# The RWKV chunk stage's preparation up to the directed keys, made once in the projection (hybrid retention and RWKV-7 layer, Trainium2)

## The reference, cut to what matters

```python
kk = heads(k * k_k); kk = kk * rsqrt(sum(kk * kk) + 1e-12)
u = w0[d] + tanh(wd) @ w2[d]                  # 64 -> 512, both directions
w = exp(-exp(-softplus(-u) - 0.5))            # = exp(-exp(-0.5) * sigmoid(u))
a = sigmoid(a0[d] + ad @ a2[d])
k_dir = k * (1.0 + (a - 1.0) * k_a)
# the scan takes w, k_dir, v, kk, a and r; later bonus = sum(r * k_dir * r_k) * v
```

## Time and profile before

| | us |
|---|---|
| median of 3 runs (4056.05 to 4069.73) | 4059.08 |
| the profiled execution | 4071.43 |
| its span | 4069.6 |

### The profile page before, as it was taken

How to read it: one execution, slowest core, us unless ns; L and a number is a source line. 1 busy time by engine, 2 the same in 40 slices (tenths; PEclk the granted TensorE clock), 3 DMA queues, 4 the chain that set the end, 5 groups by cost and what they waited for, 6 DMA issues and landing times. The chain is left out here.

```text
span 4069.6 us, 94464 instructions
## 1 busy us (share of the span) xinstructions
PE 3694.0 (91%) x39914; PEld 3087.6 (76%) x39914; DVE 2247.2 (55%) x3650; ACT 1892.5 (47%) x3029; POOL 671.5 (16%) x637
## 2 busy tenths in 40 slices
PE   7999999999978888888887978996699999999993
PEld 6878878888867777777776867785588888888883
DVE  5532533434337777777776865555444544454545
ACT  5533534433336666666565443332244444444443
POOL 1000000000012222222220333200011111111111
PEclk9999999999989999999999989998799999999997
DMA  7655565555442223322324366655366666666667
GB/s 260 199 188 183 179 198 155 154 157 158 149 145 73 69 78 81 81 79 74 96 65 124 111 221 225 202 168 189 134 206 217 214 217 212 214 206 214 212 212 299
DMA packets 378746, 673.49 MB, mean 165 GB/s; under 512 B 90428, under 2 KB 261540, under 8 KB 360712
## 3 DMA queue, kind: packets, MB, share of 16 engines
q1 hardware_dynamic: 351368, 580.69, 44.0%
q0 software_dynamic: 27008, 87.46, 7.4%
HBM read 524.89 MB, written 143.15 MB: 164 GB/s over the span
## 5 line engine op out<-in xcount | busy, mean ns | idle before, releaser
L113 PE MATMUL fro__acc<-fro__hT_hi,fro__wh 128*128 128x512 f32 (+1 forms) x1608 | 624.9, 389 | 11.8 <-DVE fro__hT_lo L2695 8.9
L114 PE MATMUL fro__acc<-fro__hT_hi,fro__wl 128*128 128x512 f32 (+1 forms) x1608 | 612.9, 381 | 0.0
L115 PE MATMUL fro__acc<-fro__hT_lo,fro__wh 128*128 128x512 f32 (+1 forms) x1608 | 612.8, 381 | 0.0
L2112 DVE TENSOR_TENSOR fin__wl<-fin__raw,fin__wh 128x4096 fp32r<-128x4096 f32 x96 | 424.7, 4424 | 316.8 <-ACT fin__wh L2056 316.8
L2701 DVE TENSOR_TENSOR fro__wl<-prj__w,fro__wh 128x1024 fp32r<-128x1024 f32 x201 | 246.3, 1225 | 637.6 <-ACT fro__wh L2484 637.6
L2056 ACT ACTIVATE fin__wh<-fin__raw 128x4096 fp32r<-128x4096 f32 x96 | 348.4, 3629 | 190.8 <-PE exp__acc L115 190.3
L113 PE MATMUL exp__acc<-fin__wh,exp__xh 128*128 128x512 f32 x1024 | 399.9, 390 | 0.8 <-DVE exp__xl L2117 0.8
L115 PE MATMUL exp__acc<-fin__wl,exp__xh 128*128 128x512 f32 x1024 | 398.5, 389 | 0.0
L114 PE MATMUL exp__acc<-fin__wh,exp__xl 128*128 128x512 f32 x1024 | 398.4, 389 | 0.0
L113 PEld LDWEIGHTS fro__acc<-fro__hT_hi,fro__wh 128*128 128x128 f32 x1608 | 303.7, 189 | 77.7 <-issue 22.2
L114 PEld LDWEIGHTS fro__acc<-fro__hT_hi,fro__wl 128*128 128x128 f32 x1608 | 303.8, 189 | 59.1 <-issue 3.6
(11 more groups left out here) (462 smaller groups left out, 7570.1 us busy)
## 6 DMA issues: line engine op xcount, KB each, us to landing
fin__raw<-in_w_x SPq DMA_DIRECT2D x96, 2048.0 KB
prj__w<-in_w_z SPq DMA_DIRECT2D x201, 512.0 KB, 4.1
s_zT<-fro__pool SPq DMA_DIRECT2D x128, 256.0 KB, 4.5
fro__wm<-in_w_mod POOLq DMA_DIRECT2D x16, 1024.0 KB, 5.8
mix__gate<-s_zT SPq DMA_DIRECT2D x64, 256.0 KB, 4.2
prj__xin<-in_tokens SPq DMA_DIRECT2D x18, 512.0 KB, 5.7
rwc__kS<-s_kS SPq DMA_DIRECT2D x36, 256.0 KB, 3.1
rwc__kkn<-s_kkn SPq DMA_DIRECT2D x36, 256.0 KB, 3.3
```

The source lines that it names most:

```text
L113: pe.matmul(out, sh, mh, start=first, stop=False)
L114: pe.matmul(out, sl, mh, start=False, stop=False)
L115: return pe.matmul(out, sh, ml, start=False, stop=last)
L2112: ve.tensor_tensor(wl[s][:, :, :], raw[s][:, :, :], wh[s][:, :, :], ALU.subtract).then_inc(w_lo, 1)
```

## The change

The low-rank products, sigmoids, directed keys, removal rows and the bonus product are made in the projection, on whole key tiles, and stored in HBM for both directions: sg, bb, kd and bon, each 2 x 512 x tokens. kS, kka, rrk and waS are no longer stored. `low_rank` makes, per key tile and direction, three fp32r products (high by high, low by high, high by low) for the decay on rows 0 to 63 and for the rate on rows 64 to 127, by turns; a 513th column is made as fp32. `rates` takes the sigmoids with a bias, `unit` makes kd, bb and bon. The tile order puts wa first and keys and queries by turns; zo has three buffers instead of four; XY buffers are held until their last reader.

The chunk stage has three load buffers (LB = 3) and loads sg, bb, kd, kkn, rS and vS in three parts each, with the upper halves exchanged, and bon whole: 19 DMAs per slab. Beta and kappa are one full-width product each. `carried` moves from DVE to POOL, in six operations on half the partitions. What is left out below are names, semaphores, the eighth early weight buffer in two parts (pool and hv) and the split of the low-rank weights.

```diff
-        ld = [{n: sb(f"{n}{d}", [P, 4, C]) for n in names} for d in range(2)]
+        each_way, both_ways = ("sg", "bb", "kd", "bon"), ("kkn", "rS", "vS")
+        ld = [{n: sb(f"{n}{u}", [P, 4, C]) for n in each_way + both_ways} for u in range(LB)]
...
             def load(j):
-                sp.dma_start(wS[d][0:64, :], T["waS"][0:64, ds(c, C)]).then_inc(lws[d], 16)
-                sp.dma_start(aS[d][0:64, :], T["waS"][64:128, ds(c, C)]).then_inc(lws[d], 16)
-                for n in names:
-                    rows = T[n][:, ds(c, C)].rearrange("(q p) t -> p q t", p=P)
-                    if n != "vS":
-                        sp.dma_start(ld[d][n][:, :, :], rows).then_inc(lds[d], 16)
+                u, c = j % LB, slab_at(j)
+                for n in each_way + both_ways:
+                    rows = (T[n][j % 2] if n in each_way else T[n])[:, ds(c, C)].rearrange("(q p) t -> p q t", p=P)
+                    landed = lsg[u] if n == "sg" else lds[u]
+                    if n == "bon":
+                        sp.dma_start(ld[u][n][:, :, :], rows).then_inc(landed, 16)
                         continue
-                    sp.dma_start(ld[d][n][0:HC, :, :], rows[0:HC, :, :]).then_inc(lds[d], 16)
+                    sp.dma_start(ld[u][n][0:HC, :, :], rows[0:HC, :, :]).then_inc(landed, 16)
                     for s in range(2):
-                        sp.dma_start(ld[d][n][HC:P, :, side(s)], rows[HC:P, :, side(1 - s)]).then_inc(lds[d], 16)
+                        sp.dma_start(ld[u][n][HC:P, :, side(s)], rows[HC:P, :, side(1 - s)]).then_inc(landed, 16)
...
+            sp.dma_start(scanm[:, :, :], T["scanm"]).then_inc(scan_in, 16)
             load(0)
...
-            load(1)
+            for u in range(1, LB):
+                load(u)
             for h in range(SLABS + 3):
-                if h + 2 < SLABS:
-                    for n in ("am", "kd1", "kd2", "bd", "al", "rho", "bonp", "trm"):
+                if h + LB < SLABS:
+                    for n in ("dd2", "betad", "kappad", "al", "rho", "trm", "bonm"):
                         sp.wait_ge(S[n], at(n, h))
-                    load(h + 2)
+                    load(h + LB)
                 if h < SLABS:
                     store_bonus(h)
...
+            def carried(j):
+                d = j % 2
+                gp.wait_ge(S["dd"], at("dd", j))
...
+                for e in range(2):
+                    upto, after = halves(L)[side(e), :, :, 31], halves(D)[side(e), :, :, HC - 1]
+                    enter, leave = (upto, after) if d == 0 else (after, upto)
+                    s, o = turn_of(j, 0) ^ e, turn_of(j, 1) ^ e
+                    gp.tensor_tensor(fl[side(e), 0, :], enter[:, :, s], dl[d][side(e), :], ALU.add)
+                    last = gp.tensor_tensor(fl[side(e), 1, :], enter[:, :, o], leave[:, :, s], ALU.add)
+                    ways.append(leave[:, :, o])
+                last.then_inc(S["fld"], 1)
+                gp.wait_ge(S["fld"], at("fld", j))
+                for e in range(2):
+                    last = gp.tensor_copy(dl[d][side(e), :], ways[e])
+                last.then_inc(S["dld"], 1)
...
+                gp.wait_ge(lds[j % LB], 16 * NLD * (j // LB + 1) + START)
+                gp.wait_ge(S["dld"], at("dld", j))
...
-            def decays(j):
-                act.wait_ge(S["um"], at("um", j))
-                if j:
-                    act.wait_ge(S["dd2"], at("dd2", j - 1))
-                act.activation(sg[:, :, :], f4(PB[1]), ACT.Sigmoid).then_inc(S["sgu"], 1)
...
-                if h + 2 < SLABS:
-                    decays(h + 2)
...
-                if h + 2 < SLABS:
-                    learning(h + 2)
...
+                ve.wait_ge(lsg[j % LB], 16 * NSG * (j // LB + 1) + START)
...
-            def key1(j):
-                ve.scalar_tensor_tensor(kd[:, :, :], av[:, :, :], -1.0, ld[j % 2]["kka"][:, :, :], ALU.add, ALU.mult).then_inc(S["kd1"], 1)
...
-                tt(D2[:, :, :], D[:, :, :], sg[:, :, :], ALU.subtract).then_inc(S["dd2"], 1)
-            def removal(j):
-                ve.scalar_tensor_tensor(bb[:, :, :], av[:, :, :], -1.0, ld[j % 2]["kkn"][:, :, :], ALU.mult, ALU.mult).then_inc(S["bd"], 1)
...
+                tt(D2[:, :, :], D[:, :, :], ld[j % LB]["sg"][:, :, :], ALU.subtract).then_inc(S["dd2"], 1)
...
+            def scaled_removal(j):
+                ve.wait_ge(lds[j % LB], 16 * NLD * (j // LB + 1) + START)
                 ve.wait_ge(S["ebk"], at("ebk", j))
-                tt(beta[0:HC, :, :], bb[0:HC, :, :], e_bk[0:HC, :, :], ALU.mult)
-
-            def scaled(j):
-                ve.wait_ge(S["kd2"], at("kd2", j))
-                for out, rows, signal in ((beta, bb, "betad"), (kappa, kd, "kappad")):
-                    if out is kappa:
-                        tt(out[0:HC, :, :], rows[0:HC, :, :], e_bk[0:HC, :, :], ALU.mult)
-                    for s in range(2):
-                        ins = tt(out[HC:P, :, side(s)], rows[HC:P, :, side(1 - s)], e_bk[HC:P, :, side(1 - s)], ALU.mult)
-                    ins.then_inc(S[signal], 1)
+                tt(beta[:, :, :], ld[j % LB]["bb"][:, :, :], e_bk[:, :, :], ALU.mult).then_inc(S["betad"], 1)
+
+            def scaled_keys(j):
+                tt(kappa[:, :, :], ld[j % LB]["kd"][:, :, :], e_bk[:, :, :], ALU.mult).then_inc(S["kappad"], 1)
...
-                    scaled(n)
-                    carried(n)
+                    scaled_keys(n)
...
-                else:
-                    pe.wait_ge(S["asg"], at("asg", min(j + 3, LAST)))
-                    if j:
-                        pe.wait_ge(S["yc1"], at("yc1", j - 1))
+                elif j:
+                    pe.wait_ge(S["yc1"], at("yc1", j - 1))
...
-                if h + 2 < SLABS:
-                    decays(h + 2)
...
-                if h + 2 < SLABS:
-                    learning(h + 2)
...
+    uses = sorted([(s + 4, s, 0) for s in keys_of] + [(s + 4 + q, s, q) for s in gate_of for q in range(4)]
+                  + [(s + 5 + x, s, "01t"[x]) for s in keys_of for x in range(2 + wide[s])], key=lambda use: use[0])
     use_of = {(s, q): i for i, (_, s, q) in enumerate(uses)}
+    assert len({use[0] for use in uses}) == len(uses)
...
-        pool = sb("pool", [P, 4 * 512 + 4 * 2 * 516 + 10 * 513])
-        zo = [pool[:, 512 * u:512 * u + 512] for u in range(4)]
+        pool = sb("pool", [P, 3 * 512 + 4 * 2 * 516 + 12 * 513])
+        zo = [pool[:, 512 * u:512 * u + 512] for u in range(3)]
...
+                        gp.wait_ge(read, rated(t))
+                        for d in range(2):
+                            gp.dma_start(turned_ways["sg"][d][ORDER[t][3], :, at:at + end - j0], sg[d][:, 0:end - j0]).then_inc(sg_out[d], 16)
...
+                        gp.wait_ge(kd_ok, i + 1)
+                        gp.dma_start(turned_ways["kd"][d][p, :, at:at + end - j0], kb[u][:, 0:end - j0]).then_inc(kb_out[u], 16)
+                        gp.wait_ge(bb_ok, i + 1)
+                        gp.dma_start(turned_ways["bb"][d][p, :, at:at + end - j0], av[d][:, 0:end - j0]).then_inc(bb_out[d], 16)
+                        if b:
+                            gp.wait_ge(bon_ok, i - 7)
+                            gp.dma_start(turned_ways["bon"][d][p, :, at:at + end - j0], kb[1][:, 0:end - j0]).then_inc(kb_out[1], 16)
...
+                        act.wait_ge(kd_ok, 2 * keys_of[old] + 2)
+                    if old in quer_of:
+                        act.wait_ge(bon_ok, 2 * quer_of[old] + 2)
+                    if old in wa_of:
+                        act.wait_ge(rank_ok, wa_of[old] + 1)
...
+            def rates(t, kind):
...
+                act.wait_ge(summed, use_of[t, kind] + 1)
+                for d in ((0, 1) if kind == "t" else (int(kind),)):
+                    for x, (out, stored) in enumerate(((sg[d], sg_out[d]), (av[d], bb_out[d]))):
+                        if kind == "t":
+                            ins = act.activation(out[:, 512:513], rc[:, x, d:d + 1], ACT.Sigmoid, bias=low_b[:, x, d, p:p + 1])
+                            continue
+                        if c:
+                            act.wait_ge(stored, 16 * c)
+                        ins = act.activation(out[:, 0:m], rc[:, x, 0:m], ACT.Sigmoid, bias=low_b[:, x, d, p:p + 1])
+                ins.then_inc(read, 1)
...
+            def low_rank(t, kind):
...
+                for d in ((0, 1) if kind == "t" else (int(kind),)):
+                    hi, lo = [w[:, d, p * P:(p + 1) * P] for w in (low_hi, low_lo)]
+                    for i, (stat, mov) in enumerate(((hi, rank_hi), (lo, rank_hi), (hi, rank_lo))):
+                        for x in range(2):
+                            own = slice(64 * x, 64 * x + 64)
+                            if kind == "t":
+                                mm = pe.matmul(rc[:, x, d:d + 1], stat[own, :].bitcast(F32), mov[own, 512:513].bitcast(F32), start=i == 0, stop=i == 2)
+                                continue
```

(38 more changed lines are left out.)

316 lines of the change are left out of this document (137 added, 179 removed).

## The result

The changed kernel takes 4228.0 us (median of 4 runs, 4224.25 to 4234.39); the kernel before, 4060.96 us beside it (4 runs, 4056.05 to 4069.73). The ratio is 1.041, with a 95% interval from 1.0388 to 1.0433. Forecast were 4184 us and a range from 4085 to 4265.

A forecast was written before the change was run, and what follows sets the result against it. TensorE bounds the projection; in the chunk stage no engine is full, and each slab would become a cycle SP to ACT to TensorE of 30.0 us. Chunk stage +95 and projection +30 make +125 on 4059: 4184 us, range 4085 to 4265.

The forecast's parts named there:

- The signs that the prediction named for the chunk stage: Chunk stage: 19 issues from the bonus copy, yo copy 17 us or more behind, TensorE gap about 5 us, clock under 1.00.
- some 30 us longer: Projection: the next profile would show TensorE still at 100% and the projection longer by this much.
- The load: SP's queue in the chunk stage: 19 issues per slab take 12.4 us plus 0.9 for slow ones, 13.3.
- The rest up to the yo copy: SP's queue behind the load: bonus store 0.55, second y store 0.8, landing 2.7, then 0.1 to the copy.
- The clock: TensorE in the chunk stage: 5.3 us idle, then 2.4 us at half rate, 1.4 us lost per slab.
- The remaining stretch: Chunk stage, yo copy to next bonus copy: 13.9 - 3.2 us, plus 0.4 for the mean slab.
- The gain per slab: Chunk stage: removed work behind the yo copy saves 1.6, 0.9 and 0.7 us, sum 3.2; unhindered slab 23.4.
- faster: Rival, SP's queue: yo stores land before ACT needs them, slab 23.4 us, total 3986; chance 0.13.
- The group of six: Projection, latent key tiles: low-rank products on alternate row halves overlap, taking half, 23 us; bounds 23 and 46.
- The tails: Projection, four tiles with a 513th column: 12 one-column products of 0.14 us, halved 0.8 per tile, 3 in all.
- The context: Projection, context block: 3 us of TensorE or more if DVE is late; taken as 4, bounds 3 and 9.
- row halves take turns without overlap: Rival, projection: low-rank products on the row halves do not overlap, +26 us, 4168 to 4210; chance 0.08.

The follow-up runs named there:

- before_long_load: The kernel before with a load of 20 issues in place of 10 that also waits for the bonus matmuls, nothing computed otherwise: 4304.05 us.
- stores_first: The changed kernel with SP issuing the two y stores of the earlier slabs ahead of the load: 4031.05 us, ratio to the kernel before 0.9888.
- load_whole: The changed kernel with each load tensor fetched by one issue, not three (7 per slab, not 19), the exchange of sides left out: 4013.39 us.
- idle_filled: The changed kernel with the kept-state matmuls moved behind level 3's doubling and issued 13 times to fill TensorE's idle stretch: 4209.36 us, ratio 1.0341.
- units_first: The changed kernel with DVE making the context keys' rate units ahead of the next weight split and the shift: 4225.80 us, ratio 1.0376.
- halves_in_series: The changed kernel with each low-rank group's three products of one row half first, then the other three, not by turns: 4222.17 us.

## Why the prediction was right, and where it was not

**Right, by its own steps.** SP's issues begin with the bonus copy (0.07 us behind it), the y stores stand behind them, ACT is stopped at the yo copy, TensorE goes idle behind ACT, and its clock falls. The signs that the prediction named for the chunk stage are all in the profile; the one for the projection, "some 30 us longer", is not. before_long_load shows that SP's queue makes the loss by itself, stores_first and load_whole that without it the stage is shorter than before.

**The whole.** Forecast was +125 us; measured are +156 between the two profiled executions and +167 between the medians. Of the 31 us missed between the executions, 12 are the context and 20 the latent blocks, 8 the slabs; 9 go the other way, most of them scatter at the start.

**The slab, term by term.** Forecast was 30.0 us, measured 30.5, and the closeness is in part luck: four terms are off and offset each other.
- The load was put at 13.3 us and takes 15.2. Its base was right, 12.4 or 19 x 0.65; the allowance for slow single issues, 0.9, is 2.8 here (kkn's first takes 1.28, the pair of rS 2.24).
- The rest up to the yo copy was put at 4.2 and is 3.5; the landing was taken as 2.7 and is 2.1.
- The clock was put at 1.4 and is worth 0.8 in the slab, 1.1 in its stretch. The gap was put at 5.3 us and the lower level at 2.4; they are 6.9 and about 3.8. So the fall was deeper than forecast and the price lower.
- The remaining stretch was 13.9 - 3.2 = 10.7 at full clock, and 0.4 for the mean slab, 11.1 in all; idle_filled has 10.7. Where nothing waits it is longer, 12.0 in stores_first and 11.2 in load_whole, for then the engines beside ACT get no time to catch up (that reason is argued, not shown).

**The gain per slab** was put at 3.2 us and is 2.9 (26.86 against 24.01). The rival "faster" (3986) named the right place and the right condition; stores_first meets it and gives 4031, beside 4078 for the kernel before, so -47 us where the rival had -73: its stage is 88 us shorter than before and not some 100, and its projection costs 61 us more and not 30.

**The projection was wrong: +30 forecast, +62 measured in context and latent blocks.** Three terms were mis-sized:
- The group of six. "I take half: 6 x 0.24 x 16 tiles = 23" had the overlap right and left out the change between full and half height. The step into a group is 0.32 us in place of 0.23 (748.94 to 749.26), the first step in it 0.34, the step out 0.33, the first full-height step 0.34: each of the four has 0.1 us too much. A group so costs 1.10 us and not 0.72: 32 groups are 35, not 23. All 32 latent groups of the changed kernel have these steps, to within 0.003 us. The wait for a semaphore at a group's first weights is not the reason: in the window 150:1173, 109 steps between full-height products have such a wait too and take 0.23. The Trainium skill (TensorEngine Tiling (Array Packing), section "Key Properties") says that changing the tiling mode drains TensorE, with no figure; the trace agrees at the steps in and out, and shows that the step behind each is longer as well.
- The tails: 1.6 us each and not 0.8, some 6.5 us for four. The prediction had the 12 products of both directions, but at half of 0.14 each; the six steps of four records (24 records, two for each fp32 product) take 0.22 to 0.30 us, and the change of height comes on top.
- The context: "I take 4, bounds 3 and 9", measured 16, or 12 to 16 with the scatter. The held XY buffer was named as a risk and not priced by itself. ACT's eviction is late twice by 3.37 us, and each time ACT's root, which now stands ahead of TensorE's low-rank products in the same step, comes late too: TensorE waits 2.98 us for it. units_first takes back 5.6 to 7.9.

Some 4 us of the latent blocks' 46 are not traced one by one; the last context key's products, which fall behind the first 512-column one, are among them.

The rival "row halves take turns without overlap" came near to the total with its +26 us and is wrong in its mechanism: the halves overlap.

## What to carry to other kernels

In this stage the queue's length was in issues, not in bytes: 19 issues held SP for 15.2 us, 7 with the same bytes for 5.1. Before cutting loads in pieces or delaying their first wait, add up the issues of one period, and look at which small store stands behind them and which buffer it frees. Put stores that free a buffer ahead of a long load. When work moves to an engine that is full, count what surrounds it too: the change of array height, and who now waits within the same step for an engine that used to have slack.

## What the runs showed of the hardware that was not expected

- Products on the two row halves pair up whatever their order in the program. Three and three take 0.91 us, six by turns 0.90, in all 32 latent groups of either kernel. The Trainium skill (TensorE: Matmul & The Clock Gate, section "The mechanism") says that matmuls start and end strictly in program order; in halves_in_series the records show the fourth product of the program starting with the first and ahead of the second, and the group's time agrees with them.
- A DMA over a part of a tensor costs SP no less than one over the whole, about 0.65 us (changed kernel) against 0.50 to 0.55 (load_whole); single issues of either kind take 1.3 us and more. The Trainium skill (DMA: Bandwidth & Descriptors, section "Issuing engines are not separate DMA queues") calls the sequencer's time for an issue usually small beside the DMA itself. For one DMA that agrees with this trace (about 0.6 us for a y store that lands after 2.0 or more); the sum does not stay small: 19 issues took 15.2 us of a slab of 30.5, at a DMA share of 0.30.
- A gap of 6.9 us and about 3.8 us at 1.2 GHz behind it cost only 0.8 us per slab (idle_filled), less than the 1.9 that TensorE alone would lose by that estimate. That the engines beside it absorb the rest is argued, not shown.
